# Two-layer modulation sums on GpSimd instead of VectorE, in a Trainium2 kernel of a deep mixed block

## The reference, cut to what matters

```
c_act = silu(c)
for l in range(2):
    mod = c_act @ w_ada[l] + b_ada[l]              # [1024] @ [1024, 6144]
    sh1, sc1, gt1, sh2, sc2, gt2 = split(mod, 6)
    h = x * (1 + sc1) + sh1
    y = token_mixer(h, ...)                        # h @ w_in[l], three attentions, gates
    x = layernorm(ALPHA * x + gt1 * y)
    h = x * (1 + sc2) + sh2
    y = conv_ffn(h, ...)                           # up (1024 -> 2 x 2816), convolution, gelu, down
    x = layernorm(ALPHA * x + gt2 * y)
```

## Time and profile before

| | |
|---|---|
| runs | 2841.63, 2843.75, 2836.32 us |
| the profiled execution, its own time | 2837.39 us |
| its span | 2835.5 us |
| mean granted TensorE clock, share of full speed | 0.959 |
| HBM traffic | 665 MB read, 4.2 MB written |

### The profile page before, as it was taken

How to read it: one execution, slowest core, us unless ns; L and a number is a source line. 1 busy time by engine, 2 the same in 40 slices (tenths; PEclk the granted TensorE clock), 3 DMA queues, 4 the chain that set the end, 5 groups by cost and what they waited for, 6 DMA issues and landing times.

```text
span 2835.5 us, 36425 instructions
## 1 busy us (share of the span) xinstructions
PE 2619.1 (92%) x13906; PEld 2223.9 (78%) x13906; DVE 2163.9 (76%) x2718; ACT 1526.3 (54%) x1806; POOL 24.1 (1%) x46
## 2 busy tenths in 40 slices
PE   7889889898998889989989988899999999999997
PEld 6667769876777779868979976788888888888885
DVE  6777677778766777666766566798988989898896
ACT  2344444434344345436534345577777777777773
POOL 0000000000000000000000000000000000000000
PEclk8999999999999999999999999799999999999998
DMA  9744336576643455443125671599989999998994
GB/s 356 279 145 146 134 134 236 196 294 253 218 138 133 154 187 209 162 155 107 56 77 199 174 249 68 212 363 348 371 342 369 344 351 364 348 372 342 369 345 177
DMA packets 104753, 671.66 MB, mean 237 GB/s; under 512 B 11984, under 2 KB 12240, under 8 KB 27136
## 3 DMA queue, kind: packets, MB, share of 16 engines
q1 hardware_dynamic: 97584, 622.08, 59.1%
q0 software_dynamic: 6992, 47.19, 4.9%
HBM read 665.03 MB, written 4.19 MB: 236 GB/s over the span
## 4 chain that ended last, share of the span: by engine, by line
PE 66%; DVE 22%; ACT 5%; issue 4%; DMA 2%; PEld 0%; DVEq 0%; SPq 0%; ACTq 0%; PEldq 0%
PE bank L852 20%; PE bank L854 19%; PE bank L853 19%; DVE W_low L2275 8%; ACT W_high L1749 2%; PE bank L1287 2%; DVE work L2360 1%; DVE arena L2265 1%; PE bank L1629 1%; DMA W<-in_w_middle 1%; DMA W<-in_w_layer 1%; DVE work L2592 1%; DMA arena<-in_w_layer 1%; DVE acted L2575 1%; DVE work L2590 1%
## 5 line engine op out<-in xcount | busy, mean ns | idle before, releaser
L2275 DVE TENSOR_TENSOR W_low<-W,W_high 128x1024 fp32r<-128x1024 f32 x426 | 496.6, 1207 | 290.3 <-ACT W_high L1749 284.5
L1749 ACT ACTIVATE W_high<-W 128x1024 fp32r<-128x1024 f32 x426 | 421.8, 1039 | 406.8 <-PE bank L854 192.8
L853 PE MATMUL bank<-W_low,arena_parts 128*128 128x512 f32 (+1 forms) x1128 | 444.6, 394 | 0.0
L852 PE MATMUL bank<-W_high,arena_parts 128*128 128x512 f32 (+1 forms) x984 | 396.7, 403 | 23.9 <-DVE W_low L2275 13.6
L854 PE MATMUL bank<-W_high,arena_parts 128*128 128x512 f32 (+1 forms) x984 | 388.8, 395 | 0.0
L854 PE MATMUL bank<-hT_high,W_low 128*128 128x256 f32 (+2 forms) x1208 | 347.9, 288 | 0.0
L852 PE MATMUL bank<-hT_high,W_high 128*128 128x256 f32 (+1 forms) x1088 | 316.6, 291 | 26.8 <-DVE W_low L2275 18.7
L853 PE MATMUL bank<-hT_low,W_high 128*128 128x256 f32 (+1 forms) x1088 | 311.2, 286 | 0.0
L852 PE MATMUL bank<-W_high,hT_high 128*128 128x512 f32 (+1 forms) x640 | 263.1, 411 | 25.2 <-DVE W_low L2275 10.7
L852 PE MATMUL bank<-arena_parts 128*128 128x512 f32 x672 | 269.3, 401 | 1.5 <-issue 1.5
L853 PE MATMUL bank<-W_low,hT_high 128*128 128x512 f32 (+1 forms) x672 | 266.4, 397 | 0.0
(11 more groups left out here) (429 smaller groups left out, 4769.7 us busy)
## 6 DMA issues: line engine op xcount, KB each, us to landing
W<-in_w_layer SPq DMA_DIRECT2D x170, 1024.0 KB, 4.9
W<-in_w_expert SPq DMA_DIRECT2D x148, 1024.0 KB, 4.9
arena<-in_w_expert SPq DMA_DIRECT2D x114, 1024.0 KB, 4.9
W<-in_w_middle SPq DMA_DIRECT2D x58, 1024.0 KB, 4.9
arena<-in_w_layer POOLq DMA_DIRECT2D x40, 1024.0 KB, 7.6
consts<-in_w_expert SPq DMA_DIRECT2D x37, 1024.0 KB, 5.0
R<-in_w_expert SPq DMA_DIRECT2D x37, 1024.0 KB, 5.1
R<-in_rows_layer SPq DMA_DIRECT2D x70, 256.0 KB, 5.7
```

The costliest lines, as they stand in the source:

```text
L852: mm(bank, lhs[0], rhs[0], start=start, stop=False)
L853: mm(bank, lhs[0], rhs[1], start=False, stop=False)
L1749: do(high_slot(at, w)[:, cols], raw(at, w)[:, cols], ACT.Copy).then_inc(main_highs.filled[main_highs.slot(at, w)], 1)
L2275: tt(lows(at, w)[:, cols], raw(at, w)[:, cols], high_slot(at, w)[:, cols].bitcast(F32), ALU.subtract).then_inc(*low_ready.event(at))
```

## The change

The sums of chunks 4 to 11 and of the four `next` chunks go to GpSimd's program, beside its loads. Since each half tile is handled there as four scalings (three or four of them in place, in the slot) and then three or four additions, each waiting for the one before, a chunk is 8 TENSOR_SCALAR and 7 TENSOR_TENSOR. GpSimd issues the load two half tiles ahead when it has given a slot back. In layer 0 it begins once the front sums are made; in layer 1 once layer 0's last normalisation is. VectorE loses `first_steps` and `ada_steps`. TensorE takes chunks 4 to 7 after n = 2 to 5, chunks 8 and 9 in units 0 and 2, and the first `next` chunk at c = 1. `ada_in(10)` comes after VectorE's tile 14.

```
@@ block.gpsimd, new
+            def load_ada(at, name):
+                pool.wait_ge(*adas.vacant(at, name))
+                n = W_LOADS[at.part].index(name)
+                pool.dma_start(ada_slots[:, adas.slot(at, name), :], ins["w_" + at.part][n]
+                               ).then_inc(*adas.fills(at, name))
+            def sum_chunk(at, chunk_, acc, more):
+                for half in range(2):
+                    w = chunk_ + (half,)
+                    pool.wait_ge(*adas.full(at, w))
+                    part = ada_slots[:, adas.slot(at, w), :].rearrange("p (k n) -> p k n", k=4)
+                    for k in range(4):
+                        f = 4 * half + k
+                        d = acc if f == 0 else part[:, k, :]
+                        pool_ts(d, part[:, k, :], csil[:, f:f + 1], None, ALU.mult).then_inc(pool_done, 1)
+                        pooled.count()
+                    pool.wait_ge(pool_done, pooled.n)
+                    for k in range(4):
+                        if 4 * half + k:
+                            pool_tt(acc, acc, part[:, k, :], ALU.add).then_inc(pool_done, 1)
+                            pool.wait_ge(pool_done, pooled.count())
+                    pool.nop().then_inc(*adas.frees(at, w))
+                    if half:
+                        pool.nop().then_inc(*ada_ready.event(at))
+                    after = ADA_LOADS[at.part].index(w) + 2
+                    if after < len(ADA_LOADS[at.part]) and ADA_LOADS[at.part][after][:2] not in (("ada", 10),):
+                        load_ada(at, ADA_LOADS[at.part][after])
...
+                if p == LAYERS[0]:
+                    pool.wait_ge(*ada_ready.nth(at, len(FRONT_SUMS)))
+                else:
+                    pool.wait_ge(*h_ready.nth(Pass(LAYERS[0]), 8))
+                for c in range(4, 10):
+                    acc = work[:, c % 2 * 512:c % 2 * 512 + 512]
+                    if c > 5 or p == LAYERS[0] and c == 5:
+                        pool.wait_ge(*psum.full(at, ("ada", c - 2)))
+                    sum_chunk(at, ("ada", c), acc, c < 9)
+                pool.wait_ge(*group_split.nth(at, 20))
+                chunks = [("ada", 10), ("ada", 11)] + [("next", c) for c in NEXT if p != LAYERS[-1]]
+                for name in ADA_LOADS[p][12:14]:
+                    load_ada(at, name)
+                for m, chunk_ in enumerate(chunks):
+                    if m > 1:
+                        pool.wait_ge(*psum.full(at, chunks[m - 2] if m < 4 else ("next", m - 4)))
+                    sum_chunk(at, chunk_, ada_acc[:, m % 2, :], m < len(chunks) - 1)
@@ block.tensor
-                    if n in (1, 3, 4, 5):
+                    if n > 1:
                         hand_back()
-                        {1: ada_row, 3: ada_row}.get(n, ada_column)({1: 4, 3: 5, 4: 6, 5: 7}[n])
+                        (ada_row if n < 4 else ada_column)(n + 2)
...
-                        if u == 4:
+                        if u in (0, 2):
                             hand_back()
-                            ada_column(9)
+                            ada_column(8 + u // 2)
...
-                    if l + 1 < DEPTH and c in (0, 3, 6, 8):
+                    if l + 1 < DEPTH and c in (1, 3, 6, 8):
                         next_column((c + 1) // 3)
@@ block.vector
-                    low(1)
-                    sums(3)
-                    low(1)
+                    low(2)
                     take_chunk(kind, c, lambda t: z[:, t, c * 512:(c + 1) * 512], ready)
-                    if n in (1, 3, 4, 5):
-                        ada_in({1: 4, 3: 5, 4: 6, 5: 7}[n])
-                    sums(3 if n else 5)
+                    if n > 1:
+                        ada_in(n + 2)
...
-                    for _ in range(2 if j > 13 and j % 2 else 1):
-                        next(steps_, None)
-                    if j == 17:
+                    if j == 14:
                         ada_in(10)
```

More of the change, by code:

```diff
@@ L806, in _ @@
             sp.wait_ge(out_written, 32)
[L809 to L829, removed]
         @block.tensor
@@ L1718, in _ @@
                     expert(i, False)
+        @block.gpsimd
+        def _(pool):
+            pooled = Steps()
+            pool_ts, pool_tt = nc.gpsimd.tensor_scalar, nc.gpsimd.tensor_tensor
+            def load_ada(at, name):
[24 more added lines that the diff above has]
+                        load_ada(at, ADA_LOADS[at.part][after])
+            for s in weights.freed + stream.freed + main_highs.freed + adas.freed + rows.freed + psum.freed:
+                pool.sem_inc(s, 1)
+            for p in LAYERS:
+                at = Pass(p)
+                if p == LAYERS[0]:
+                    pool.wait_ge(*weights.full(at, ("A", 0, 0)))
+                for name in ADA_LOADS[p][0:2]:
+                    load_ada(at, name)
+                if p == LAYERS[0]:
+                    pool.wait_ge(*ada_ready.nth(at, len(FRONT_SUMS)))
[9 more added lines that the diff above has]
+                for name in ADA_LOADS[p][12:14]:
+                    load_ada(at, name)
+                for m, chunk_ in enumerate(chunks):
+                    if m > 1:
+                        pool.wait_ge(*psum.full(at, chunks[m - 2] if m < 4 else ("next", m - 4)))
+                    sum_chunk(at, chunk_, ada_acc[:, m % 2, :], m < len(chunks) - 1)
+            at = Pass("middle")
+            pool.wait_ge(*bias_made.nth(at, 1))
+            pool.dma_start(spread, relrow[0:WQ_HEADS, :].unsqueeze(1).to_broadcast([WQ_HEADS, P, 384])
+                           ).then_inc(bias_out, 16)
+            pool.wait_ge(bias_out, 16)
+            shifted = bass.AP(spread.tensor, P - 1, [[383, P], [P * 384, WQ_HEADS], [1, S]])
+            pool.dma_start(wbias, shifted).then_inc(bias_in, 16)
@@ L2674, in take_chunk @@
                     dve.nop().then_inc(*rows.frees(v.at, (kind, c)))
-                first = first_steps()
-                def sums(n):
-                    for _ in range(n):
-                        next(first, None)
                 for n in range(6):
@@ L2700, in _ @@
                 low(1)
-                sums(2)
                 dve.wait_ge(*rows.full(v.at, ("bf", 0)))
@@ L2710, in _ @@
                 low(1)
-                ada_in(8)
                 def background():
@@ L2808, in _ @@
                     dve.wait_ge(*probs.last(v.at))
-                    if u == 4:
-                        ada_in(9)
+                    if u in (1, 3):
+                        ada_in(8 + u // 2)
                     if u % 2 == 0:
@@ L2814, in _ @@
                         a_out(u - 1)
-                    if u < 4:
-                        sums(2)
                     low(1)
@@ L3006, in _ @@
                 shifted_rows("h2T", modc[:, 64:72], modc[:, 72:80], keep_taps)
-                steps_ = ada_steps(l)
                 def between_up(j):
@@ L3022, in _ @@
                     low(1)
-                    for _ in range(3):
-                        next(steps_, None)
                     if c == 0 and l + 1 < DEPTH:
@@ L3029, in _ @@
                         dve.wait_ge(*rows.vacated(v.at, ("nextc", 0)))
-                    if l + 1 < DEPTH and c in (1, 5, 8):
+                    if l + 1 < DEPTH and c in (2, 5, 8):
                         next_in(c // 3)
```

45 lines of the change are left out of this document (1 added, 44 removed).

## The result

| | before | changed |
|---|---|---|
| median, us | 2842.69 (4 runs, 2836.32 to 2845.27) | 2982.19 (4 runs, 2974.62 to 2983.83) |
| the profiled execution | 2837.39, span 2835.5 | 2981.56, span 2979.7 |
| mean granted clock | 0.959 | 0.941 |

A forecast was written before the change was run, and what follows sets the result against it. TensorE, busy 92% of the span, was taken as the bound, in the up stage a VectorE and ScalarE loop. 30 + 23 - 10.9 - 5.8 + 6 = +42 us on 2837.4 gave 2880 us, range 2802 to 2912.

The forecast's parts named there:

- What GpSimd's sum costs: GpSimd's price per chunk: scalings at 0.75 us, adds at 1.2, two load issues, 15.5 us together; bounds 9.7 and 19.1.
- upper bound: GpSimd's dearest case: each of 15 instructions takes 1.2 us, half a VectorE lowering pair, so 19.1 us a chunk.
- The fronts: Front stages of both layers: GpSimd finishes chunk 9 17 us late in layer 0, 13 in layer 1; sum +30.
- The exclusion: GpSimd's SBUF reads and VectorE's instructions with two SBUF tensors block each other; 42 us of blocking per front.
- The up stages: Three two-operand VectorE instructions per tile each wait 0.4 us; 3.9 us a chunk, six chunks, +23.
- The re-timing: Earlier `ada_in(10)` in the up stages saves 10.9 us, the earlier first `next` column in the down stage 5.8.
- The down stage: Layer 0: `next` chunks of 25 us each on GpSimd, the fourth ready at 637 against 630 wanted; +6.
- Rival 3: Exclusion with GpSimd at 19.1 us a chunk: both fronts end 22 us later each than forecast, 2925 or more; chance 0.06.
- Rivals 1 and 2: First: no exclusion beyond double-rate instructions, 2804, chance 0.28. Second: exclusion, GpSimd near its lower bound, 2815 to 2840, 0.12.
- Rival 4: GpSimd's half-tile loads wait behind its arithmetic and come late, shrinking the no-exclusion gain to 2822; within that case's 0.28.

The follow-up runs named there:

- e5: The changed kernel with the sums of chunks 10, 11 and `next` back on VectorE, re-timings kept: 2929.27 us, ratio 1.0301.
- e1: The kernel before with only the change's two re-timings, all sums staying on VectorE: 2830.56 us, ratio 0.9967.
- e3: The kernel before plus 40 column scalings of 128x512 on GpSimd beside layer 0's up stage, on unused memory: 2849.07 us, ratio 1.0024.
- e12: The kernel before plus 40 adds of two 128x512 tensors on GpSimd beside layer 0's up stage, each waited for: 2860.36 us, ratio 1.0074.
- e4: The kernel before plus 40 memsets of 128x512 on GpSimd beside layer 0's up stage, on unused memory: 2843.03 us, ratio 1.0005.
- e7: The changed kernel with every second scaling left out, so its output is not the reference's: 2886.77 us, ratio 1.0161.
- e8: The changed kernel with a wait for completion on GpSimd behind every scaling: 2977.79 us, ratio 1.0477.
- e2: The kernel before plus 40 GpSimd instructions of five forms beside layer 0's up stage, on unused memory, each waited for: 2848.15 us in one execution.

## Why the prediction was wrong

- **The section "What GpSimd's sum costs" failed, in its scaling.** "One element per cycle for the scalings, the 0.75 of a sum step", with 1.2 us as the upper bound: GpSimd takes 1.56. The bound itself was none, since it rested on an instruction of another engine; the 1.2 for the add was right (1.26). Also not counted were 0.6 us ahead of each load's issue. A chunk alone is 23.7 us and not 15.5, over the 19.1 of the upper bound, and above the 19.7 at which TensorE's own pace lies, so that every chunk was late and not the last ones.
- **The fronts** were given +30 and cost +97 (e5 against e1). By the prediction's own steps: six chunks dearer by 8.2 us are 49 us per front. The exclusion was overrated there, at 42 us per front: 210.6 - 43.9 - 6 x 23.7 leaves 24.5. For layer 0 that gives 17 + 49 - 17.5 and 2.4 for the later start, 51; for layer 1 13 + 49 - 17 = 45. Measured 51.4 and 45.8.
- **The up stages** were given +23 on top of the re-timing's gain. Against e1 the tiles cost 26.4 in layer 0 and 12.5 in layer 1, together 39: 6.5 us a chunk, not 3.9. That two engines exclude each other held, but not as put there: an instruction met was to wait half of the running one, alike for both kinds of GpSimd instruction. A lowering that met an add waited for its end, and e3 and e12 show 0.07 us per scaling and 0.51 per add. The Trainium skill, "SBUF — State Buffer", section "Who interferes with whom", has a VectorE instruction with two SBUF inputs contend with a GpSimd instruction that reads SBUF, and not with one that only writes; memsets (e4) and adds (e12) agree. By the same section whoever holds the shared ports blocks the other for its whole instruction. For the adds of e12 the trace agrees (18 of 18 lowerings waited for the add's end). For scalings it doesn't: in e3 seven lowerings began 0.64 to 0.72 us into one, and neither engine's instruction was lengthened.
- **The re-timing** was given 10.9 + 5.8 = 16.7 us and brought 9.3 (e1). In layer 0 7.9 of 12.0 came back, in layer 1 only 1.7 of 4.8: the 3.40 us wait at 1160 vanished without its worth.
- **The down stage** was given +6, with chunks of 25 us. Layer 0's pair of stages is 42.5 us longer than e1's, 26.4 of it in the up stage: 16 are left for the down stage. Its cause is the chunk again, 23.7 us alone: GpSimd's last two take from 656.58 to 714.18, 57.6 us, and not 50, and from c = 3 to c = 8 TensorE takes 46.5 us (29.9 in before).
- **The rivals.** Rival 3, the upper bound of the price, named the mechanism and the size "2925 or more", with a chance of 0.06 and beyond the end of the stated range, 2912; its price, too, was passed. Rivals 1 and 2 needed a chunk below 19.7 and 12 us. Rival 4, late loads, didn't come up: GpSimd waited for a load three times, 10.77 us ahead of its very first chunk and 8.74 and 8.50 ahead of the first half of chunk 10 in either layer, never from one chunk to the next in the fronts.
- e7 is the nearest to a test of the other terms: with a chunk of about the price that was taken, the loss is 45.6 against 42. But this agreement is partly of errors that cancel: its fronts cost 10 us each (17 and 13 forecast), its up and down stages with the re-timing +17.8 and +8.3, where the prediction's terms make about +10 and +3.

Left open: why GpSimd's TENSOR_SCALAR is dearer than a product of two tensors, and why an add holds VectorE up to its end and a scaling, as it seems, only in its first part. That the number of memory operands decides is a guess: no run here changed it for one and the same operation. Open is also how far the up stages' 6.5 us a chunk split between adds and scalings, and why layer 1's front is 6 us longer in e5 and e8 than in the changed kernel, while layer 0's is about the same.

## What to carry to other kernels

Before work is moved to an engine that has done none of its kind in the trace, let it do forty such instructions beside the old kernel, on unused memory: a bound from another engine's instruction is none. Idle time of an engine is worth nothing if one unit of the work takes longer there than the one who waits for it needs; here TensorE came every 19.7 us, and in e7 a chunk of 17.5 us alone still cost 10 us in each front. And look whether a change's small re-timings pay alone: here they were its only gain.

## What was unexpected of the hardware

- On GpSimd a 128x512 float32 TENSOR_SCALAR takes 1.49 us with a constant and 1.56 with a column, the product with a broadcast column 1.04 to 1.1, an add 1.04 (one tensor twice) to 1.26 (two), a copy 0.61, a memset 0.52. The copies of e2 never became longer beside VectorE (610 to 612 ns); the others did, a memset up to 0.77 us and a scaling up to 3.7.
- GpSimd's instructions don't hold up VectorE's alike: 40 adds lengthened the up stage by 20.5 us, 40 scalings by 3.0. A lowering waited for a running add to its end; seven that began 0.64 to 0.72 us into a scaling (e3) weren't held up.
- Behind its own arithmetic a load's issue on GpSimd took 0.61 us in the median (at most 0.70), with 0.6 us of idle time before it, where it took 0.53 in before.
